# Two gate tiles ahead of attention instead of three, and eight more conv taps split between ScalarE and GpSimd

## The reference

```
for l in range(2):
    h = rmsnorm(x, norm_mix[l])
    q, k, v, u, ug, ga, gb = split(h @ w_in[l])          # 16 query heads, 2 key heads, 64 wide
    q, k = partial_rope(rmsnorm(q)), partial_rope(rmsnorm(k))
    a_out = sliding_window_attention(q, k, v, sinks[l])  # window 128, blocks of 128 queries
    a = u * sigmoid(ug)                                  # 512 channels
    y = causal depthwise conv of a, 31 taps, + conv_b    # y[t] = sum_j w[j] a[t - 30 + j]
    c_out = silu(layernorm(y)) @ w_conv_out[l]
    x = x + (sigmoid(ga) * a_out + sigmoid(gb) * c_out) @ w_out[l]
    x = x + (silu(g) * up) @ w_down[l]                   # g, up = split(rmsnorm(x) @ w_gate_up[l])
```

## Time and profile before

| | |
|---|---|
| median of 3 runs | 2346.22 us (2346.11 to 2350.28) |
| the profiled execution's own time | 2346.27 us |
| its span, first to last instruction | 2344.5 us |
| TensorE busy | 2280.5 us (97%) |
| VectorE, ScalarE, GpSimd busy | 1172.3 us (50%), 990.9 us (42%), 969.1 us (41%) |
| mean granted clock of TensorE | 0.991 |

### The profile page before, as it was taken

The page is one execution under the profiler, slowest core; times in us unless marked ns, Lnnn a source line. Parts: engine busy times, 40 slices in busy tenths (PEclk is TensorE's granted clock), DMA queues, the critical chain, the costliest instruction groups (busy, mean ns, idle before and its releaser), DMA issues.

```text
span 2344.5 us, 29244 instructions
## 1 busy us (share of the span) xinstructions
PE 2280.5 (97%) x10560; PEld 1794.3 (77%) x10560; DVE 1172.3 (50%) x1483; ACT 990.9 (42%) x1497; POOL 969.1 (41%) x445
## 2 busy tenths in 40 slices
PE   6999999999999999999999999999998999999999
PEld 5866678888888876678888888876776667888887
DVE  5876664222344786665222333747897443433300
ACT  4546643333214545744333213324535664444311
POOL 4962234444443982234444442432331113444442
PEclk9999999999999999999999999999999999999999
DMA  4221122333662221122333572321221002333322
GB/s 151 88 66 55 61 74 90 98 98 95 194 212 81 85 78 45 56 71 91 98 98 98 168 235 72 99 76 60 63 81 45 28 28 72 100 97 98 99 91 88
DMA packets 59843, 216.01 MB, mean 92 GB/s; under 512 B 6640, under 2 KB 6896, under 8 KB 59760
## 3 DMA queue, kind: packets, MB, share of 16 engines
q1 hardware_dynamic: 52272, 187.62, 26.0%
q10 hardware_dynamic: 7488, 27.27, 3.5%
HBM read 212.76 MB, written 2.10 MB: 92 GB/s over the span
## 4 chain that ended last, share of the span: by engine, by line
PE 56%; issue 22%; DVE 9%; POOL 9%; ACT 3%; DMA 0%; POOLq 0%; SPq 0%; DVEq 0%; ACTq 0%
PE bank L1258 16%; PE bank L1260 16%; PE bank L1259 16%; POOL wl L306 9%; DVE tmp L1152 2%; PE bank L1711 1%; PE bank L1715 1%; PE bank L1392 1%; PE bank L1452 1%; PE bank L1332 1%; PE bank L1699 1%; PE bank L1327 1%; PE bank L1432 1%; ACT prob L465 1%; DVE k L1154 1%
## 5 line engine op out<-in xcount | busy, mean ns | idle before, releaser
L306 POOL TENSOR_TENSOR wl<-raw,wh 128x1024 fp32r<-128x1024 f32 x351 | 853.0, 2431 | 1336.1 <-ACT wh L366 1336.1
L1258 PE MATMUL bank<-hh,wh 128*128 128x512 f32 x2024 | 815.8, 403 | 33.7 <-DVE hl L744 19.3
L1260 PE MATMUL bank<-hh,wl 128*128 128x512 f32 x2024 | 794.1, 392 | 0.0
L1259 PE MATMUL bank<-hl,wh 128*128 128x512 f32 x2024 | 793.9, 392 | 0.0
L366 ACT ACTIVATE wh<-raw 128x1024 fp32r<-128x1024 f32 x351 | 369.7, 1053 | 628.1 <-PE bank L1260 601.8
L1258 PEld LDWEIGHTS bank<-hh,wh 128*128 128x128 f32 x2024 | 383.3, 189 | 130.2 <-issue 29.7
L1259 PEld LDWEIGHTS bank<-hl,wh 128*128 128x128 f32 x2024 | 383.7, 190 | 85.7 <-issue 8.9
L1260 PEld LDWEIGHTS bank<-hh,wl 128*128 128x128 f32 x2024 | 383.3, 189 | 81.6
L1258 PE MATMUL bank<-ah,wh 128*128 (+1 forms) x528 | 208.0, 394 | 0.0
L1260 PE MATMUL bank<-ah,wl 128*128 (+1 forms) x528 | 207.0, 392 | 0.0
L1259 PE MATMUL bank<-al,wh 128*128 (+1 forms) x528 | 204.9, 388 | 0.0
(11 more groups left out here) (317 smaller groups left out, 2600.3 us busy)
## 6 DMA issues: line engine op xcount, KB each, us to landing
raw<-stream SPq DMA_DIRECT2D x351, 512.0 KB, 3.6
ada_w<-ada ACTq DMA_DIRECT2D x48, 512.0 KB, 4.7
x<-x_t ACTq DMA_DIRECT2D x4, 512.0 KB, 7.8
out_t<-x SPq DMA_DIRECT2D x8, 256.0 KB, 2.1
cst<-consts SPq DMA_DIRECT2D x1, 640.0 KB, 11.3
tmp<-masks SPq DMA_DIRECT2D x1, 320.0 KB, 11.6
par<-params SPq DMA_DIRECT2D x1, 253.0 KB, 4.7
cst<-consts SPq DMA_DIRECT2D x1, 224.0 KB, 8.1
```

The costliest lines, as they stand in the source:

```text
L306: nc.gpsimd.tensor_tensor(wl[:, slot, :], raw[:, raw_slot, :], wh[:, slot, :].bitcast(F32), ALU.subtract).then_inc(lo_ready, 1)
L1258: mm(dst, wh[:, slot, w], xh, start=start, stop=False)
L1259: mm(dst, wh[:, slot, w], xl, start=False, stop=False)
L1260: return mm(dst, wl[:, slot, w], xh, start=False, stop=stop)
```

## The change

One gate tile moves from ahead of the attention into it: tiles 0 and 1 stand before `scores(0)`, tile 2 behind it, and tile 3 in group 0, so that each of groups 0 to 12 has one (g + 3). From group 1 on TensorE's order is as before.

`SPLIT` goes from 16 to 24: eight more taps of conv tile 0 are ScalarE products and GpSimd additions, and VectorE has 69 taps of its own in a layer instead of 77. The pieces of VectorE's taps are shared out anew, so that one tap is left behind the read of gate tile 1, where five stood there and three behind the read of gate tile 2. ScalarE has 55 products and GpSimd 53 additions where they had 47 and 45. The last nine products stand in three pieces: five in a row ahead of `exps(0)`, two behind gate tile 2 and two behind gate tile 3 in group 0; before, the last three stood in two pieces, both ahead of `exps(0)`. GpSimd's last additions stand behind the subtraction of weight tile 9 of the gates (`ADDS_AT[C_GATE + 5]`).

The diff (left out are only lines that rename `EARLY_GATES` to its value):

```
-        EARLY_GATES = 3
-        CO_FROM = 16 - EARLY_GATES
+        EARLY_GATES = 2
+        CO_FROM = 13
...
-        TAPS_U, TAPS_Q = [2, 3, 4, 4, 4, 4], [4, 4, 3, 3, 5, 5, 5, 5]
-        SPLIT, LN_EARLY = 16, 2
+        TAPS_U, TAPS_Q = [2, 3, 2, 0, 5, 5], [5, 4, 3, 4, 5, 5, 6, 6]
+        SPLIT, LN_EARLY = 24, 2
...
-        PRODUCTS_AT = {2: 3, C_K: 2, C_Q: 4, C_V: 2, C_GATE: 2, C_GATE + 1: 2, C_GATE + 2: 1}
+        PRODUCTS_AT = {2: 3, C_K: 2, C_Q: 4, C_V: 4, C_GATE: 2, C_GATE + 1: 3, C_GATE + 2: 2, C_GATE + 3: 2, C_GATE + 4: 2}
...
-        ADDS_AT = {2: 1, C_K: 2, C_V: 2, C_GATE: 2, C_GATE + 1: 2, C_GATE + 2: 2}
+        ADDS_AT = {2: 1, C_K: 2, C_V: 4, C_GATE: 2, C_GATE + 1: 2, C_GATE + 2: 2, C_GATE + 3: 2, C_GATE + 4: 2, C_GATE + 5: 2}
... in ScalarE's program
+                products(C_GATE + 2)
                 exps(0)
+                gate(2)
+                products(C_GATE + 3)
                 for g in range(16):
...
                     else:
-                        gate(g + EARLY_GATES)
+                        gate(g + 3)
+                        if g == 0:
+                            products(C_GATE + 4)
... in VectorE's program
-                taps(5)
+                taps(4)
                 gate(1, M_V % 4)
-                taps(5)
-                gate(2, M_SWAP[7] % 4)
                 taps(len(own) - tapped[0])
                 join_split()
...
                 maxima(0)
+                gate(2, 6)
                 normalise(0)
... in TensorE's program
-                tile(c0 + C_GATE + 2, (c0 + C_GATE + 2) % RW, M_SWAP[7] % 4, hh, hl)
...
                 scores(0)
-                pe.wait_ge(conv_ready, (CT - 1) * l + 2)
-                tile(c0 + C_GATE + EARLY_GATES, (c0 + C_GATE + EARLY_GATES) % RW, 6, hh, hl)
+                pe.wait_ge(conv_ready, (CT - 1) * l + 1)
+                tile(c0 + C_GATE + 2, (c0 + C_GATE + 2) % RW, 6, hh, hl)
...
-                    if 1 <= g < CO_FROM:
-                        pe.wait_ge(gate_free, 16 * l + g + EARLY_GATES)
-                        c = c0 + C_GATE + g + EARLY_GATES
-                        tile(c, c % RW, 6, hh, hl)
-                    if g >= CO_FROM:
-                        out(2 * (g - CO_FROM) + 1, 6)
                     if g == 0:
                         pe.wait_ge(conv_ready, (CT - 1) * (l + 1))
+                    if g < CO_FROM:
+                        pe.wait_ge(gate_free, 16 * l + g + 3)
+                        c = c0 + C_GATE + g + 3
+                        tile(c, c % RW, 6, hh, hl)
+                    else:
+                        out(2 * (g - CO_FROM) + 1, 6)
```

More of the change, by code:

```diff
@@ L946, in _ @@
                                 out_rest(t)
-                        gate(g + EARLY_GATES, 6)
+                        gate(g + 3, 6)
                     else:
```

## The result

The changed kernel took 2358.48 us (median of 7 runs, 2356.26 to 2361.93) where the kernel before took 2349.06 (7 runs, 2346.11 to 2352.45): a ratio of 1.0042, 95% interval 1.0033 to 1.0052. That is 9.9 us of 2349.06, so the changed kernel is slower, and by more than 0.2%. In the profiled executions the span went from 2344.5 to 2356.6 us and the mean granted clock from 0.991 to 0.986.

A forecast was written before the change was run, and what follows sets the result against it. TensorE was taken to bound the kernel, so only its idle time could change. Group 1 8.2, additions 2.0, clock -1.6 and +1.2 sum to 9.8 us; 2346.27 + 9.8 = 2356.1 us, range 2351 to 2361.

The forecast's parts named there:

- What bounds: TensorE is busy 2280.5 of 2344.5 us, so the change acts only through its idle time; 11.5 us could be won.
- Costs nothing: Up to the end of gate tile 1 all stays as it is, with at most one or two 0.8 us taps added.
- TensorE arrives earlier, first wait: Start of attention: the conv wait goes, five products delay the first exps, and TensorE waits 3.2 us for the first probabilities.
- Group 0: TensorE waits 0.8 us before pv and 1.7 us before the second transposes; 5.7 us of waits for 5.75 so far.
- Group 1: TensorE waits 2.9 us before the second pv, 1.3 us before the third transposes; 4.1 us lost a layer, 8.2 in both.
- Additions inside the groups: GpSimd's additions in groups 2 and 3 delay the probabilities of groups 3 and 4; 1.0 us a layer, 2.0 in both.
- The clock: Second layer's slow stretch, 1.6 us, is won back; new falls behind long waits cost 0 to 3.2 us, taken as 1.2.
- the slots don't hold ScalarE up: Rival: group 0's exps start at 159, TensorE waits 0.85 us for them; faster, 2334.9 us; chance 0.10.
- they hold it up once only: Rival: GpSimd far enough ahead in group 1, waits of 3.2, 0.8 and 1.7 us remain; 2345 or 2346 us; chance 0.10.
- The deeper loss: Rival: the lock also delays group 3 and four long waits each halve the clock behind them; 2365 us; chance 0.12.

The follow-up runs named there:

- short additions: The changed kernel with its last four additions a layer on 8 columns of 512; one run, profile alone used: wait at the mean's matmul 1.4 us.
- eight slots: The changed kernel with eight slots for the products in place of four; ratio 0.9964 to the kernel before, 2340.12 us.
- gate tiles only: The kernel before with only the gate tiles moved, its tables of taps, products and additions kept; ratio 0.9993 to the kernel before, 2346.19 us.

## Why the prediction was right, point by point

- *What bounds.* The prediction let the change act through TensorE's idle time alone. It acted through waits and through the slower clock behind them. The loss lies in the two attentions: 8.03 + 4.82 = 12.9 us in the profiled executions, whose spans differ by 12.1.
- *Costs nothing.* TensorE has no wait between the first tiles and the attention, as said. That ScalarE would be held three times a layer there too was not foreseen; it had the time.
- *TensorE arrives earlier, first wait.* Predicted 3.2 us for the first probabilities; 3.13 in both layers. The last of five products waited for addition 45, and the exps followed at once.
- *Group 0.* Predicted waits of 0.8 and 1.7 us, measured 0 and 0.79. ScalarE's and GpSimd's times were as worked out (3.78 us of idle time, then 0.71), but gate tile 3 ran behind the first wait at 1.2 GHz (163.58 to 170.46, 6.9 us with the way to pv, not 5.6) and filled them. The second transposes came 0.26 us earlier than before; 0.1 was predicted.
- *Group 1.* Predicted 2.9 us before the second pv; 2.86. The 1.3 us before the third transposes did not show as a wait: the clock was low there too, and pv and scores took 4.2 us (182.91 to 187.12) in place of 2.6. Lateness at the third transposes: 4.1 predicted (its own times, 188.55 less 184.51, give 4.04), 4.24 and 4.13 measured (the second with the 1.57 of before).
- *Additions inside the groups.* 1.0 us a layer taken, 0.69 and 0.80 measured, and shown by the short additions (one execution) to be theirs. The rule of the Trainium skill that the prediction weighed, page SBUF — State Buffer, section on SBUF's two separate sides, is borne out by this run: without the long additions the operations are 1.22 and 0.69 us again.
- *The clock.* This is the term that was mis-sized, in place and in amount. The 1.6 us of before were won back, as said. The two long waits did let the clock fall, in both layers, but the slack behind them took it up. What cost time were falls behind waits of only 2 us, which I had not counted: before the mean's matmul (1.63 and 1.51 us in the two layers) and before gate tile 14 (1.50, first layer), 4.6 us in the profiled execution where 1.2 was taken. With the 1.6 won back the clock cost 3.1 us net, where the sum had a gain of 0.4 and its range ended at a loss of 1.6. It varies from one execution to the next: the 7 runs of the changed kernel had mean clocks of 0.984 to 0.989 and times of 2361.93 to 2356.26 us in that order. So the close agreement of the sum, 9.8 against 9.9 by the ratio, is in part luck: in the traces the parts come to 6.8 (for 6.6), 1.5 (for 2.0) and 4.6 (for 1.2), 12.9 us, and the execution that the sum was made against took 2346.27 us, 2.8 less than the median of all runs of before, and the changed kernel's profiled one took 2358.48, 12.2 more.
- *Rivals.* That the slots don't hold ScalarE up fell: eight slots gave 0.9964 and the wait pattern of that rival almost to the number (about 1.1 us of waiting for the first probabilities where 0.85 was worked out). That they hold it up once only fell with the 3.81 us of the third pair. The deeper loss fell: the two attentions lost 12.9 us, not 18.6. Of its reasons one came true without its price: the clock did fall behind the long waits, but what it slowed had slack.

## What to carry to other kernels

Two engines that hand work over through a ring are coupled by its length: count for each item which earlier item frees its slot and what the other engine has in front of that one. An item that needs a release from behind work which the producer has only just handed over stops the producer for the whole of it, and everything queued behind it. So before moving work to idle engines, look at what stands behind it in their queues: here one gate tile moved, two taps moved and a rebalanced VectorE gave all of the gain, and eight taps turned it into a loss. (Which of the three the gain needs was not taken apart; the gate tile alone gave none.)

## What the runs showed of the hardware that was not expected

Waits of TensorE cost more than their length. The granted clock fell to half for 3.4 us behind waits of 1.8 to 3.1 us, not every time (the wait of 1.9 us before gate tile 14 had it in the first layer of the changed kernel and not in the second), and for some 6.7 us behind those of 4.3 us (gate tiles only, both layers) and once behind one of 3.1 us (short additions, second layer, from 880 us). Behind the 1.4 us before the mean's matmul no run had it. A fall cost 1.5 to 1.6 us where TensorE was what the rest waited for, 2.7 us for the long one, and nothing where another engine set the pace. With the waits filled by matmuls there was none up to the output projection, but new ones behind the 1.8 us wait in the output projection; that filling shortens the whole kernel was not shown.
